# Moving the transposed tiles 160 and 192 bytes further within their 256 bytes of address

## What is computed

```python
def first_block(x, ...):
    for i in range(DEPTH):
        ...
        x = _layer_norm(ALPHA * x + y, ln_mix_g[i], ln_mix_b[i])
        x = _layer_norm(ALPHA * x + _sq_relu_mlp(x, ff_w1[i], ff_w2[i]), ln_ff_g[i], ln_ff_b[i])
    return x
```

## Time and profile before

| | |
|---|---|
| median of 3 runs | 769.11 us (768.78 to 769.23) |
| the profiled execution | 769.54 us |
| its span, first to last instruction | 767.7 us |
| instructions | 12051 |
| TensorE products busy | 756.7 us, 4962 of them |
| TensorE weight loads busy | 688.3 us |
| VectorE busy | 586.2 us |
| ScalarE busy | 405.3 us |
| weights and inputs read | 173.15 MB |

### The profile page before, as it was taken

How to read it: one execution, slowest core, us unless ns; L and a number is a source line. 1 busy time by engine, 2 the same in 40 slices (tenths; PEclk the granted TensorE clock), 3 DMA queues, 4 the chain that set the end, 5 groups by cost and what they waited for, 6 DMA issues and landing times.

```text
span 767.7 us, 12051 instructions
## 1 busy us (share of the span) xinstructions
PE 756.7 (99%) x4962; PEld 688.3 (90%) x4962; DVE 586.2 (76%) x787; ACT 405.3 (53%) x513; POOL 34.5 (4%) x66
## 2 busy tenths in 40 slices
PE   8999999999999999999999999999999999999996
PEld 8999888999999889888889999998799987999985
DVE  4887898878688797788978778777678877666654
ACT  5455234545434434865345445434748968755632
POOL 0000000000000011000000000000500051000001
PEclk9999999999999999999999999999999999999999
DMA  9977548897768631456588988886226354754102
GB/s 338 383 271 277 210 157 317 330 353 292 305 242 315 257 119 63 165 171 241 169 321 328 329 283 332 320 296 242 93 92 230 113 198 169 276 215 165 55 5 80
DMA packets 27416, 174.99 MB, mean 228 GB/s; under 512 B 3297, under 2 KB 3681, under 8 KB 8289
## 3 DMA queue, kind: packets, MB, share of 16 engines
q1 hardware_dynamic: 27072, 174.19, 61.0%
q10 hardware_dynamic: 288, 0.02, 0.0%
HBM read 173.15 MB, written 1.05 MB: 227 GB/s over the span
## 4 chain that ended last, share of the span: by engine, by line
PE 96%; ACT 1%; DMA 1%; POOL 1%; DVE 0%; issue 0%; SPq 0%; POOLq 0%; ACTq 0%; DVEq 0%
PE bank L590 12%; PE bank L592 12%; PE bank L591 12%; PE Y L727 11%; PE Y L728 11%; PE Y L730 11%; PE bank L1080 2%; PE bank L1081 2%; PE bank L1082 2%; PE bank L1009 2%; PE Y L752 1%; PE bank L1046 1%; PE bank L830 1%; PE bank L656 1%; PE bank L1047 1%; PE bank L1051 1%
## 5 line engine op out<-in xcount | busy, mean ns | idle before, releaser
L1639 DVE TENSOR_TENSOR w_low<-raw,w_high 128x2048 fp32r<-128x2048 f32 (+3 forms) x124 | 277.6, 2247 | 70.6 <-ACT w_high L1222 68.2
L1222 ACT CAST w_high<-raw 128x2048 fp32r<-128x2048 f32 (+3 forms) x124 | 231.5, 1877 | 93.4 <-DMA raw<-weights 82.2
L590 PE MATMUL bank<-xT_h,w_high 128*128 128x256 f32 x720 | 201.4, 280 | 0.0
L591 PE MATMUL bank<-xT_l,w_high 128*128 128x256 f32 x720 | 200.8, 279 | 0.0
L592 PE MATMUL bank<-xT_h,w_low 128*128 128x256 f32 x720 | 200.8, 279 | 0.0
L591 PEld LDWEIGHTS bank<-xT_l,w_high 128*128 128x128 f32 x720 | 135.4, 188 | 1.1
L590 PEld LDWEIGHTS bank<-xT_h,w_high 128*128 128x128 f32 x720 | 135.3, 188 | 1.1
L592 PEld LDWEIGHTS bank<-xT_h,w_low 128*128 128x128 f32 x720 | 135.3, 188 | 0.0
L727 PE MATMUL Y<-w_high,hT_h 128*128 128x512 f32 x324 | 126.8, 391 | 0.0
L728 PE MATMUL Y<-w_low,hT_h 128*128 128x512 f32 x324 | 126.5, 390 | 0.0
L730 PE MATMUL Y<-w_high,hT_l 128*128 128x512 f32 x324 | 99.9, 390 | 0.0
(11 more groups left out here) (291 smaller groups left out, 1130.5 us busy)
## 6 DMA issues: line engine op xcount, KB each, us to landing
raw<-weights SPq DMA_DIRECT2D x149, 1024.0 KB, 5.0
rows<-rows_in SPq DMA_DIRECT2D x9, 512.0 KB, 8.0
raw<-weights SPq DMA_DIRECT2D x4, 576.0 KB, 3.6
z<-gates_in SPq DMA_DIRECT2D x4, 512.0 KB, 3.6
raw<-weights SPq DMA_DIRECT2D x2, 896.0 KB, 4.5
z<-xT_in SPq DMA_DIRECT2D x2, 512.0 KB, 5.6
raw<-weights SPq DMA_DIRECT2D x4, 256.0 KB, 6.9
raw<-weights SPq DMA_DIRECT2D x2, 512.0 KB, 7.9
```

The source lines that it names most:

```text
L590: mm(dst, high, xh[:, kt, :], start=kt == 0, stop=False)
L591: mm(dst, high, xl[:, kt, :], start=False, stop=False)
L1222: nc.scalar.copy(w_high[:, n % RING, start:COLS[n]], raw[:, s % RAW, start:COLS[n]]).then_inc(w_high_ready, 1)
L1639: tt(w_low[:, n % RING, start:COLS[n]], slot[:, start:COLS[n]], f32(w_high[:, n % RING, start:COLS[n]]), ALU.subtract).then_inc(raw_done, 1)
```

## The change

Two sizes of unused tiles. `space_1` grows from 8 to 48 columns of 4 bytes (32 to 192 bytes per partition) and `space_2` from 8 to 16 (32 to 64 bytes).

```diff
         x = sb("x", [P, TB, D])
         z = sb("z", [P, TB, D])
-        sb("space_1", [P, 8])
+        sb("space_1", [P, 48])
         xT_h = sb("xT_h", [P, KT, SEQ], F32R)
         xT_l = sb("xT_l", [P, KT, SEQ], F32R)
-        sb("space_2", [P, 8])
+        sb("space_2", [P, 16])
         stage = sb("stage", [P, 2, 512])
```

## The result

The changed kernel takes 764.96 us (median of 4 runs, 764.06 to 767.08) beside 768.97 us for the kernel before: ratio 0.995, interval 0.9938 to 0.9962. It is 4.0 us faster. The forecast was 10 us slower. The profiled execution took 765.03 us.

A forecast was written before the change was run, and what follows sets the result against it. The prediction took TensorE, busy 99%, as the bound: number of products times distance between starts. Its terms, 12.0 + 0.7 - 2.3, summed to +10.4 us, forecasting 779.5 us; range 750 to 797, the forecast's own 771 to 786.

The forecast's parts named there:

- Step (1): 2400 products with xT moving: d, moving minus stationary address modulo 256, going 32 to 192 adds 5.0 ns each, +12.0 us.
- Step (2): Queries with hT moving, 444 products: from 120.0 to 121.6 ns each, +0.7 us.
- Step (3): `down` with hT stationary, some 1000 products: unchanged at 226.7 ns, 0 us.
- Step (4): `down` with xT stationary, 342 products: 233.3 to 226.7 ns, -2.3 us; 240 products of 256 columns left at 118.3.
- Steps (5) and (6): Plain float32 products do not react to offsets; VectorE, ScalarE and SyncE's queue add nothing: 0 us each.
- Rival B: Faster: 192 is quiet for both roles, moving and stationary; -17.6 us together, 751.5 us; chance 0.32 for this side.
- its weaker form: Only `down` on hT and xT gains, xT moving stands still, queries give -1.5 us: 760.9 us.
- The sign that the prediction named for itself: Mean duration of L590 to L592 on xT, 279 ns: 284 if the forecast holds, 290, 276 or less, or 279 under rivals.
- C: Place modulo 256 does not set the distance between products: time stays at 769.1 us, chance 0.10; with 64-byte period, +5.9.

The follow-up runs named there:

- m1: Kernel of TensorE's products alone, reference computation left out: `up` and `down` at every 16th byte offset; `up` took 113.3 to 120.0 ns, at 192 either 113.3 or 117.8.
- m2: TensorE's products alone: `up` at every 4th byte offset, the ring shifted instead, 112 and 192 entered from seven kinds of work; 113.3 to 123.0 ns.
- a0: The changed kernel unaltered, profiled and timed once more: 765.54 us (764.76 to 769.13), ratio 0.9961 to the kernel before.

## Why the prediction was wrong

**Step (1), xT moving, is the one that failed.** It gave d = 192 one price, +5.0 ns, because the extra seemed to grow on that side. There are two prices, 113.3 (3.4 ns less than before) and 117.8 (1.1 more), and neither is near 121.6. Counted over the profiles of before and after, from each start to the next, they average to -1.3 ns, 2400 x -1.3 = -3.1 us in place of +12.0. The +5.0 came from joining three values as steps of a slope; the sweep shows that there is no slope: 113.3 at 112 lies between 120.0 at 96 and 118.5 at 128. The mean of `up` over all sixteen places of m1's first pass is 117.9, not 121.6. The step has a slip of its own besides: it takes the middle of 3.3, which is counted from d = 32, and 6.7, which is counted from d = 0. Counted from d = 32 both, the middle of 3.3 and 10.0 is 6.7, or +16 us, still further off. Nor does d = 32 have one price, as the 117.8 under m1 shows.

**Step (2), the queries:** +1.6 ns by the same value. Most stretches went from 120.0 to 113.3, some to 117.8; with the breaks between stretches it is -4.5 as a mean, 444 x -4.5 = -2.0 us in place of +0.7.

**Step (3), `down` on hT,** was put at 226.7 unchanged. It settles at 228.9, and over a unit of ff0 it is 229.7 against 227.7; over all, some 1000 x 1.7 = +1.7 us.

**Step (4), `down` on xT:** the direction is right, the size off: 233.3 went to 228.9, not to 226.7, -4.0 ns within a run of products; with the breaks between runs it is -0.8 us and not -2.3. The 240 of 256 columns gave 0.1 us.

**Steps (5) and (6)** hold. The other engines' busy times did not move, and TensorE's idle time rose by 0.3 us. The chain of after has VectorE and ScalarE with 3% each, so the cover looks thinner, but it was not used up.

The four terms give -4.2 us beside -4.5 in the span. Rival B had the right sign, but its mechanism, one place that is quiet for both roles, is not what the runs show, and its weaker form (760.9) let `down` gain and `up` stand still; in fact `down` on hT lost, and `up` and the queries gained. The range of 750 to 797 held the time only because it reached over both signs. The sign that the prediction named for itself would have misled: the mean duration of L590 to L592 stayed at 279, which it ascribed to C, and was the mean of two patterns. C falls by m1. What the prediction drew from the Trainium skill's rule of two independent ports ("TensorE: Matmul & The Clock Gate", Part 2, step 1), that no offset could matter, falls as well: in m2, with every other engine idle, the same product starts every 113.3 to 123.0 ns by the addresses of its operands alone. That the two reads share bandwidth, which the rule denies, is not shown by that.

What stays open is why. That the moving read and the next weight load meet is argued: the address of either changes the distance, and moving both by 32 bytes left it alone at two differences of three. No run took one of the two away. Nor is it known what in a transition picks the pattern; one late product did it in the first mixer of after, and several did not in a0.

## What to carry to other kernels

Where TensorE is the bound and runs in groups of identical products, read the distance of starts, phase by phase, before and after any change of an SBUF address: over 24 to 48 products it is exact to 0.4 ns, and a mean duration hides a split like 113.8 and 117.7. Don't extrapolate a price from one address to another; sweep it with TensorE alone, in the alternation that the kernel has, since an isolated sweep gave 226.7 for a `down` that had 228.8 in the kernel. Prefer a place that showed one pattern behind every kind of work (here xT at 112 bytes, the rings where they are) to one that is cheap only when entered well, and test the parts of a placement change together, because here they didn't add.

## What was not expected of the hardware

- Beside 106.7 ns for 256 columns, a float32r product carried 6.7 to 16.3 ns by the place of its moving operand modulo 256, the ring's staying; the least, 6.7 ns (16 cycles at 2.4 GHz), at 112 of 64 offsets in steps of 4 bytes and, in one of two patterns, at 192. With 512 columns it was 13.3 to 30.0 and never less.
- At 192 bytes the same stream ran at 113.3 or at 117.8 ns, in one case over thirteen rounds of 72 products (some 140 us). In one profile four products inserted once moved it to the other for the eleven rounds left, and in another two distances of 224 and 223 ns in a stream of 113.3 did so for the 190 products left.
- Moving one operand by 4 bytes, from 112 to 116, cost 8.5 ns a product (113.3 to 121.8).
